# Routed experts: rows gathered for two experts at once by split products, slot weights applied in gate times up, scatter unweighted, output written in two parts

## Chip, cores and metric

The kernel runs on one core of a Trainium2 chip. The metric is the device time of one execution in microseconds (us), as the median of several runs; lower is better. One further execution is profiled, and all rows below come from it.

## What is computed

Two blocks of two layers each, on 256 rows (tokens) of 1024 channels, all in float32. The change touches only the last piece, the mixture of experts in the second layer of the second block:

```python
def moe_swiglu(h, w_router, b_router, w_gate, w_up, w_down):
    t = h.reshape(B * S, D)                                  # 256 x 1024
    logits = (t @ w_router) + b_router                       # 8 experts
    top_val, top_idx = lax.top_k(logits, TOP_K)              # 2 per row
    top_w = jax.nn.softmax(top_val, axis=-1)
    combine = jnp.sum(jax.nn.one_hot(top_idx, N_EXPERTS) * top_w[..., None], axis=1)
    out = jnp.zeros_like(t)
    for e in range(N_EXPERTS):
        out = out + combine[:, e:e + 1] * swiglu(t, w_gate[e], w_up[e], w_down[e])
    return out                                               # swiglu: (silu(h@gate) * (h@up)) @ down, width 3584

x = x + g2[:, None, :] * f                                   # f is out of above
```

## The kernel before

**Products.** Most large products are split: an operand x is kept as hi = x rounded to the type fp32r (ACT copies it) and lo = x - hi (DVE subtracts), and a product is the sum of three matrix products in that type, hi\*hi + hi\*lo + lo\*hi (`mm3`). Products of plain float32 operands are written as one `mm`; the trace has two MATMUL records for each of these and one for each product of fp32r operands.

**Weights.** They come in chunks of 1 MB through a ring (SP issues the loads, six chunks ahead). Each chunk has two halves. For a half, ACT makes `whi` (`act_split`, L954), then DVE makes `wlo` (`dve_split`, L1349), then PE multiplies. There are four buffers of halves, so ACT can start a half only when PE has finished the one four places earlier.

**The routed part** begins after the router. DVE works out for each row its two experts, its weights (`cmb`) and its place (`pos`) among the rows of each expert, at most 128 (`CAP`) an expert; the largest count decides at a branch (`fork`) whether the routed code below or the code for all rows runs. With the inputs used, the routed code runs. PE meanwhile turns the rows (`hn`, L927) and ACT copies them to `HN`. Then come the eight experts `e`, each with seven steps `f` (step n = 7e + f, 56 in all). On PE a step is, in this order:

- `hidden(n, "gate")`: 24 products of 512 columns into bank 0 or 2,
- `turn(n - 1)`: four transposes (L2015) of the hidden values of the step before,
- `hidden(n, "up")`: 24 products, into bank 1 or 3,
- what is extra in some steps: `turn_weights` in n = 2, 4, 6, 8, `scatter(e - 1)` in f = 2, `gather(e + 1)` in f = 4,
- `down(n - 1)`: 24 products into banks 4 and 5, which collect over the seven steps of an expert.

ACT does silu of gate (L2093) and the hi of the turned values (L2098), DVE multiplies by up (L2177) and makes the lo (L2170). In the first steps DVE also builds the matrices of the gather, `PSEL` (`select`, L2132: 1 where a row stands in a slot), and of the scatter, `PW` (`weigh`, L2138: the same times the weight `cmb`), which PE turns to `PWT`.

`gather(e)` picks an expert's rows: 16 float32 products of 128 columns, `HN` by `PSEL`, in two groups (banks 6 and 7); ACT makes the hi `XGH` (L2080) and DVE the lo `XGL` (L2146) of each. At the end of an expert ACT copies bank 4 and DVE bank 5 to `YS` (L2117, L2194), side by side. `scatter(e)` puts the results back in the rows' places: 8 float32 products of 256 columns, `YS` by `PWT`, in four groups that take banks 6 and 7 in turn, and DVE adds each group to `FACC` (L2154 for the first expert, L2157 after). After the last scatter DVE multiplies `FACC` by the gate of the layer and adds it to `xT` (L2198), and ACT issues four stores.

The order on each engine is the order of the code; a wait stops all that stands behind it on its engine.

## Time and profile before

| | |
|---|---|
| time, median of 3 runs | 2358.19 us (2356.99 to 2359.99) |
| the profiled execution | 2358.97 us, of which its span 2357.2 us |
| PE busy (matmul) | 2218.2 us, 94% of the span |
| DVE busy | 1784.1 us, 76% |
| ACT busy | 1393.6 us, 59% |
| the routed part | from about 1285 us to the end |
| in it, 1810 to 1940 us: PE, DVE, ACT busy | 128.8, 110.3, 93.3 of 130 us |
| there: granted PE clock, share of DMA engines, rate | 1.00, 0.87, 335 GB/s |

A row of the time line has the start (us from the span's start), the duration, the engine, the source line, the operation, what is written and what is read, and how many records are merged into the row; in square brackets stands how long the engine was idle before it and who ended that. A matrix product's record is longer than its turn on PE, as products overlap: two starts, one after the other, give the pace.

### The profile page before, as it was taken

Reading aid. Unit: us, or ns where it says so; the run is one execution under the profiler, and the core shown is the slowest. Engines: PE = TensorE matmul, PEld = TensorE weight load, DVE = VectorE, ACT = ScalarE, POOL = GpSimd, SP = SyncE. Lnnn points to the kernel's source line nnn. Section 1 sums busy time; section 2 is a strip of 40 time slices with the busy share of each in tenths; the row PEclk is TensorE's granted clock in tenths of the full one; section 3 lists DMA queues with packets and bytes.
Section 4 is the critical chain, followed back from the end, with each engine's and each line's share of the span. In section 5 each row is a group of like instructions: output and inputs, shape, how many; then the busy total and the mean of one; then the engine's idle time right before and its main releaser. Section 6 shows DMA issues by size and latency. Waiting matters only on the chain.

```text
span 2357.2 us, 31258 instructions
## 1 busy us (share of the span) xinstructions
PE 2218.2 (94%) x12766; PEld 1917.4 (81%) x12766; DVE 1784.1 (76%) x2276; ACT 1393.6 (59%) x1960; POOL 2.2 (0%) x17
## 2 busy tenths in 40 slices
PE   6989998998998988999988999999999999999998
PEld 6779998877998878999777777777777777777776
DVE  6567776756877845766846888888888888888887
ACT  4345544445544745444745767776777777776775
POOL 0000000000000000000000000000000000000000
PEclk9789999889999989999998999999999999999999
DMA  6336655434666413767413988898988888898985
GB/s 238 119 116 226 242 207 206 162 118 159 238 213 229 170 54 125 249 211 255 171 36 126 344 319 334 320 359 308 356 334 329 335 335 335 332 355 311 349 338 191
DMA packets 89428, 574.88 MB, mean 244 GB/s; under 512 B 10048, under 2 KB 10176, under 8 KB 31040
## 3 DMA queue, kind: packets, MB, share of 16 engines
q1 hardware_dynamic: 87984, 566.89, 64.4%
q0 software_dynamic: 288, 3.15, 0.4%
q10 hardware_dynamic: 1008, 2.79, 0.3%
q8 instruction: 102, 1.67, 0.3%
q14 instruction: 46, 0.38, 0.0%
HBM read 571.75 MB, written 1.05 MB: 243 GB/s over the span
## 4 chain that ended last, share of the span: by engine, by line
PE 71%; DVE 15%; ACT 10%; issue 2%; DMA 1%; SPq 0%; DVEq 0%; ACTq 0%
PE bank L458 37%; PE bank L1973 34%; DVE wlo L1349 8%; ACT whi L954 4%; DVE side L1442 2%; ACT arena L2093 1%; ACT hsh L2098 1%; DVE arena L1681 1%; DVE RSTD L1411 1%; DMA ring<-in_w_in 1%; DVE XC L1399 1%; ACT arena L1181 0%; DMA side<-in_w_ada 0%; ACT midh L1170 0%; DVE XC L1377 0%
## 5 line engine op out<-in xcount | busy, mean ns | idle before, releaser
L1349 DVE TENSOR_TENSOR wlo<-ring,whi 128x1024 fp32r<-128x1024 f32 (+1 forms) x990 | 1128.5, 1187 | 116.2 <-ACT whi L954 106.0
L954 ACT ACTIVATE whi<-ring 128x1024 fp32r<-128x1024 f32 (+1 forms) x990 | 978.0, 1028 | 179.0 <-PE bank L1973 145.2
L458 PE MATMUL bank<-HH,whi 128*128 128x256 f32 x1536 | 447.0, 291 | 18.5 <-DVE wlo L1349 11.1
L458 PE MATMUL bank<-HH,wlo 128*128 128x256 f32 x1536 | 439.1, 286 | 0.0
L458 PE MATMUL bank<-HL,whi 128*128 128x256 f32 x1536 | 438.4, 285 | 0.0
L1973 PE MATMUL bank<-whi,xgh 128*128 128x512 f32 x896 | 366.0, 409 | 8.7 <-DVE wlo L1349 0.3
L1973 PE MATMUL bank<-whi,xgl 128*128 128x512 f32 x896 | 354.5, 396 | 0.0
L1973 PE MATMUL bank<-wlo,xgh 128*128 128x512 f32 x896 | 353.8, 395 | 0.0
L458 PEld LDWEIGHTS bank<-HH,whi 128*128 128x128 f32 x1536 | 297.3, 194 | 28.2 <-issue 16.9
L458 PEld LDWEIGHTS bank<-HL,whi 128*128 128x128 f32 x1536 | 297.9, 194 | 0.5
L458 PEld LDWEIGHTS bank<-HH,wlo 128*128 128x128 f32 x1536 | 297.8, 194 | 0.0
L1973 PEld LDWEIGHTS bank<-whi,xgh 128*128 128x128 f32 x896 | 168.2, 188 | 72.0 <-DVE wlo L1349 36.7
L1973 PEld LDWEIGHTS bank<-whi,xgl 128*128 128x128 f32 x896 | 167.9, 187 | 41.2
L1973 PEld LDWEIGHTS bank<-wlo,xgh 128*128 128x128 f32 x896 | 169.0, 189 | 35.2
L1973 PE MATMUL bank<-whi,hsh 128*128 128x512 f32 x448 | 181.0, 404 | 4.9 <-DVE wlo L1349 2.4
L1973 PE MATMUL bank<-whi,hsl 128*128 128x512 f32 x448 | 177.4, 396 | 0.0
L1973 PE MATMUL bank<-wlo,hsh 128*128 128x512 f32 x448 | 176.7, 394 | 0.0
L458 PE MATMUL bank<-midh,whi 128*128 128x256 f32 x528 | 150.7, 285 | 5.7 <-DVE wlo L1349 5.5
L458 PE MATMUL bank<-midl,whi 128*128 128x256 f32 x528 | 150.1, 284 | 0.0
L458 PE MATMUL bank<-midh,wlo 128*128 128x256 f32 x528 | 150.0, 284 | 0.0
L1442 DVE SCALAR_TENSOR_TENSOR side<-side,cact 128x1024 f32<-128x1024 f32 x84 | 107.5, 1280 | 7.4 <-DMA side<-in_w_ada 6.9
L1973 PEld LDWEIGHTS bank<-whi,hsh 128*128 128x128 f32 x448 | 84.1, 188 | 30.2 <-DVE wlo L1349 9.5
(261 smaller groups left out, 2581.0 us busy)
## 6 DMA issues: line engine op xcount, KB each, us to landing
ring<-in_moe_gate SPq DMA_DIRECT2D x112, 1024.0 KB, 6.3
ring<-in_moe_up SPq DMA_DIRECT2D x112, 1024.0 KB, 5.3
ring<-in_moe_down SPq DMA_DIRECT2D x112, 1024.0 KB, 5.5
side<-in_w_ada SPq DMA_DIRECT2D x96, 512.0 KB, 4.3
ring<-in_w_up SPq DMA_DIRECT2D x44, 1024.0 KB, 4.8
ring<-in_w_in SPq DMA_DIRECT2D x32, 1024.0 KB, 5.7
ring<-in_w_down SPq DMA_DIRECT2D x32, 704.0 KB, 4.6
ring<-in_ffn_gu SPq DMA_DIRECT2D x22, 1024.0 KB, 4.8
```

Source lines behind the costliest of these rows:

```text
L458: return pe.matmul(out, lhsT, rhs, start=start, stop=stop, skip_group_check=True)
L954: a.activation(hi, part, ACT.Copy).then_inc(*made.up(("hi", n, i)))
L1349: v.tensor_tensor(lo, part, hi.bitcast(F32), ALU.subtract).then_inc(*done.up(("lo", n, i)))
L1399: v.scalar_tensor_tensor(XC[:, lo:hi, :], bc(PS[BANK[s.name, "mean"]][:, 0:S], 2), -1.0 / s.kt, XC[:, lo:hi, :], ALU.mult, ALU.add).then_i ...
L1411: v.reciprocal(RSTD[:, 0, :], RSTD[:, 0, :]).then_inc(*v_norm.up((s.name, "rstd")))
L1442: v.scalar_tensor_tensor(side_acc, side_in[n % 2], cact[:, k:k + 1], side_acc, ALU.mult, ALU.add).then_inc(*v_mod.up(("acc", n)))
L1681: v.scalar_tensor_tensor(gc[:, s:S], b[:, S:512 - s], W(f"w_fconv{l}", (2 - s) * NJ + j), gc[:, s:S], ALU.mult, ALU.add).then_inc(*v_ffn.u ...
L1973: return pe.matmul(out, lhsT, rhs, start=start, stop=stop, skip_group_check=True)
L2093: a.activation(SGB[n % 2], PS[2 * (n % 2)][:, :], ACT.Silu).then_inc(*r_act.up(("silu", n)))
L2098: a.activation(flat(HSH[(n - 1) % 2][:, :, :]), PS[BANK["turn", n - 1]][:, :], ACT.Copy).then_inc(*r_hi.up(("hst", n - 1)))
```

## The change

- **Gather**: for two experts (a pair p) at once. `HN` is kept as hi `HNH` and lo `HNL` (a new helper `low_of_rows` on DVE, in HL's space), `PSEL` is written as fp32r. A group is 4 products of fp32r operands and 256 columns (two experts wide); a pair has 4 groups g of hi (x = 0) and 4 of lo (x = 1), 32 products. ACT copies the x = 0 groups to `XG[..][0]`, DVE the x = 1 groups to `XG[..][1]`. The first pair is gathered ahead of step 0, in banks 2 to 7; pair p in steps f = 3 to 6 of expert 2p - 1, one g in each.
- **Slot weights**: 4 float32 products of one column for a pair give each slot's weight (`wsl`), which goes into the product with up (L2177 becomes a `scalar_tensor_tensor`). `weigh` and `PW` go; PE turns `PSEL` itself.
- **Scatter**: `YS` becomes hi `YSH` (ACT, both banks) and lo `YSL` (DVE, both banks, each after ACT's copy), and each of the 8 products becomes two of fp32r operands and 256 columns.
- **Output**: in step f = 4 of the last expert DVE adds `FACC` of the first seven experts to `xT`; at the end it adds the last expert's rows out of the banks, without `FACC`.
- The split `HH`, `HL` of the last normed rows is made only in the code for all rows.

```diff
+            def low_of_rows(i):
+                for g in range(2):
+                    h = slice(512 * g, 512 * g + 512)
+                    v.wait_ge(*a_rout("hn", i, g))
+                    v.tensor_tensor(HNL[:, i, h], PS[BANK["hn", i, g]][:, :], HNH[:, i, h].bitcast(F32), ALU.subtract).then_inc(
+                        *v_rout.up(("hnl", i, g)))
...
+            low_of_rows(0)
             b = PS[BANK["counts",]]
             v.wait_ge(*p_rout("counts"))
...
             v.tensor_copy(icnt[:, :], cmx).then_inc(*v_rout.up(("count",)))
+            low_of_rows(1)
...
+            def gather(p, g, x, bank=None):
+                until = [(r_vec if x else r_hi, "xg", p, g, x)]
...
+                pe.wait_ge(*r_vec("select", 2 * p + 1))
...
+                for k in range(2):
                     for i in range(2):
+                        at = 128 * (2 * g + k)
+                        tm = mm(b[:, S * k:S * k + S], (HNL if x else HNH)[:, i, at:at + 128],
+                                PSEL[:, i, 2 * p:2 * p + 2, :].rearrange("p e s -> p (e s)"), i == 0, i == 1)
+                tm.then_inc(*r_mm.up(("xg", p, g, x)))
+
+            def slot_weights(p):
+                b = take("wsl", p, until=[(r_vec, "wsl", p)])
+                for e in (2 * p, 2 * p + 1):
+                    for i in range(2):
+                        tm = mm(b[:, e % 2:e % 2 + 1], PSEL[:, i, e, :].bitcast(F32), cmb[:, i, e:e + 1], i == 0, i == 1)
...
             def scatter(e):
-                pe.wait_ge(*r_act("ys", e))
-                pe.wait_ge(*r_vec("ys", e))
                 pe.wait_ge(*r_act("pwt", 6))
                 for g in range(4):
-                    b = take("facc", e, g, until=[(r_vec, "facc", e, g)])
+                    pe.wait_ge(*r_vec("ysl", e, g // 2))
+                    b = take("facc", e, g, until=[(r_vec, "facc", e, g) if e < NE - 1 else (r_vec, "out", g)])
                     for m in range(2):
                         k = 2 * g + m
-                        tm = mm(b[:, S * m:S * m + S], YS[:, 128 * k:128 * k + 128], PWT[:, e, :], True, True)
+                        mm(b[:, S * m:S * m + S], YSH[:, 128 * k:128 * k + 128], SELT[:, e, :], True, False)
+                        tm = mm(b[:, S * m:S * m + S], YSL[:, 128 * k:128 * k + 128], SELT[:, e, :], False, True)
...
-                    if f == 4 and e + 1 < NE:
-                        gather(e + 1)
+                    if f >= 3 and e % 2 == 1 and e + 1 < NE:
+                        for x in range(2):
+                            gather((e + 1) // 2, f - 3, x)
+                        if f == END:
+                            slot_weights((e + 1) // 2)
...
-                    v.tensor_tensor(SGB[n % 2], SGB[n % 2], PS[2 * (n % 2) + 1][:, :], ALU.mult).then_inc(*r_vec.up(("hs", n)))
-                    if n < NE - 1:
+                    v.scalar_tensor_tensor(SGB[n % 2], SGB[n % 2], wsl[:, e:e + 1], PS[2 * (n % 2) + 1][:, :], ALU.mult,
+                                           ALU.mult).then_inc(*r_vec.up(("hs", n)))
+                    if 0 < n < NE - 1:
                         select(n + 1)
-                    if n < NE and n % 2 == 1:
-                        weigh(n - 1)
...
+                    if f == 4 and e == NE - 1:
+                        for m in range(8):
+                            v.wait_ge(*r_vec("facc", NE - 2, m // 2))
+                            add_out(m, FACC[:, m, :]).then_inc(*r_vec.up(("part", m)))
...
-                        v.tensor_copy(YS[:, 512:1024], PS[5][:, :]).then_inc(*r_vec.up(("ys", e)))
-            scatter(NE - 1)
+                        for h in range(2):
+                            v.wait_ge(*r_act("ysh", e, h))
+                            c = slice(512 * h, 512 * h + 512)
+                            v.tensor_tensor(YSL[:, c], PS[4 + h][:, :], YSH[:, c].bitcast(F32), ALU.subtract).then_inc(
+                                *r_vec.up(("ysl", e, h)))
```

Three places as the two programs have them. First DVE around the branch, before (`small` holds the router's values, `icnt` the count that the branch reads, `XC` is where `PSEL` lay):

```order
L1877 SCALAR_TENSOR_TENSOR small<-bank2,small 128x16
L1880 TENSOR_SCALAR small<-small 128x16
L1881 TENSOR_REDUCE small<-bank2 128x1
L1883 CAST icnt<-small 128x1
L2350 TENSOR_LOAD icnt
L2351 COMPARE_AND_BRANCH
L2132 TENSOR_SCALAR XC<-cst,small 128x128 x2
L1349 TENSOR_TENSOR wlo<-ring,whi 128x1024 x2
```

and now (`HL` holds `HNL`):

```order
L1862 TENSOR_TENSOR HL<-bank6,hnh_67 128x512
L1862 TENSOR_TENSOR HL<-bank7,hnh_67 128x512
L1899 SCALAR_TENSOR_TENSOR small<-bank2,small 128x16
L1905 CAST icnt<-small 128x1
L1862 TENSOR_TENSOR HL<-bank0,hnh_67 128x512
L1862 TENSOR_TENSOR HL<-bank1,hnh_67 128x512
L2417 TENSOR_LOAD icnt
L2418 COMPARE_AND_BRANCH
L2178 TENSOR_SCALAR psel_59<-cst,small 128x128 x4
L1362 TENSOR_TENSOR wlo<-ring,whi 128x1024 x2
```

Two subtractions stand ahead of the count's work, two ahead of the branch, and four rather than two selections behind it.

On PE ahead of step 0, between the branch and the first product of gate (bank 0), before:

```order
L2351 COMPARE_AND_BRANCH
L1973 MATMUL bank6<-XC,arena 128x128 x8
L1973 MATMUL bank7<-XC,arena 128x128 x8
L1973 MATMUL bank0<-whi,xgh0_51 128x512
```

and now:

```order
L2418 COMPARE_AND_BRANCH
L1997 MATMUL bank2<-psel_59,hnh_67 128x256 x4
L1997 MATMUL bank3<-psel_59,hnh_67 128x256 x4
L1997 MATMUL bank4<-psel_59,HL 128x256 x4
L1997 MATMUL bank5<-psel_59,HL 128x256 x4
L1997 MATMUL bank6<-psel_59,hnh_67 128x256 x4
L1997 MATMUL bank7<-psel_59,hnh_67 128x256 x4
L1997 MATMUL bank6<-psel_59,HL 128x256 x4
L1997 MATMUL bank7<-psel_59,HL 128x256 x4
L1997 MATMUL bank6<-small,psel_59 128x1 x4
L1997 MATMUL bank0<-whi,xg0_55 128x512
```

All 32 products of the first pair and the four of the slot weights stand ahead of step 0; bank 6 is taken three times and bank 7 twice.

On DVE in step f = 4 of the last expert, now (before, no `xT` row stands there):

```order
L1362 TENSOR_TENSOR wlo<-ring,whi 128x1024 x4
L2227 SCALAR_TENSOR_TENSOR arena<-arena,small,bank3 128x512
L2203 SCALAR_TENSOR_TENSOR xT<-arena,modT,xT 128x256 x8
L1362 TENSOR_TENSOR wlo<-ring,whi 128x1024 x2
L1362 TENSOR_TENSOR wlo<-ring_2_65,whi 128x1024 x4
```

The eight additions stand between the product with up and the lo half of the second chunk of down.

## Rows read from the trace of the kernel before

**Rows 1.** Waits from 1290 us on: engine line, who ended it: us, times, longest.

```profile
PEld bank L1973 <- DVE wlo L1349: 46.2, 78, 1.1
```

**Rows 2.** Chain that ended last, 2300 us on: start us, us, what.

```profile
2306.47 0.60 ACT arena L2093
...
2308.53 1.24 DVE wlo L1349
...
2309.81 14.30 PE bank L1973 x60
...
2324.14 0.60 ACT arena L2093
```

**Rows 3.** Time line of PE: the transposes of steps 8 to 11.

```profile
1460.49 0.60 PE L2015 MATMUL bank<-cst,arena 128*128 128x128 f32 x4
...
1481.80 0.60 PE L2015 MATMUL bank<-cst,arena 128*128 128x128 f32 x4
...
1499.43 0.60 PE L2015 MATMUL bank<-cst,arena 128*128 128x128 f32 x4
...
1521.02 0.60 PE L2015 MATMUL bank<-cst,arena 128*128 128x128 f32 x4
```

**Rows 4.** Time line: a gather, on PE and ACT (step 11).

```profile
1505.87 3.73 PE L1973 MATMUL bank<-XC,arena 128*128 128x128 f32 x32
...
1507.86 0.60 ACT L2080 ACTIVATE xgh<-bank 128x512 fp32r<-128x512 f32 x1 [3.35 <-PE bank L1973]
```

**Rows 5.** Time line of PE: pace of fp32r products of 256 columns, full and half clock.

```profile
1256.58 0.28 PE L458 MATMUL bank<-HH,whi 128*128 128x256 f32 x1
...
1256.70 0.28 PE L458 MATMUL bank<-HL,whi 128*128 128x256 f32 x1
...
1246.48 0.41 PE L458 MATMUL bank<-HH,whi 128*128 128x256 f32 x1
1246.69 0.41 PE L458 MATMUL bank<-HL,whi 128*128 128x256 f32 x1
```

**Rows 6.** Time line: a scatter, on PE and DVE (step 9).

```profile
1466.95 3.80 PE L1973 MATMUL bank<-arena 128*128 128x256 f32 x16
...
1467.30 0.68 DVE L2177 TENSOR_TENSOR arena<-arena,bank 128x512 f32<-128x512 f32 x1
1468.01 0.69 DVE L2154 COPY arena<-bank 128x512 f32<-128x512 f32 x1
```

**Rows 7.** Time line: an early step (n = 1), PE's transposes and DVE's weighing.

```profile
1308.74 0.60 PE L2015 MATMUL bank<-cst,arena 128*128 128x128 f32 x4
...
1327.36 0.60 PE L2015 MATMUL bank<-cst,arena 128*128 128x128 f32 x4
...
1316.54 1.11 DVE L2138 TENSOR_SCALAR SQ<-cst,small 128x128 f32<-128x128 f32 x4
```

**Rows 8.** Time line: an expert's end, ACT and DVE.

```profile
1568.57 0.60 ACT L2117 ACTIVATE arena<-bank 128x512 f32<-128x512 f32 x1 [1.73 <-PE bank L1973]
1569.06 3.89 ACT L954 ACTIVATE whi<-ring 128x1024 fp32r<-128x1024 f32 x4
...
1570.14 4.63 DVE L1349 TENSOR_TENSOR wlo<-ring,whi 128x1024 fp32r<-128x1024 f32 x4 [0.89 <-ACT whi L954]
```

**Rows 9.** Time line of the start; last row a stretch: us, busy us by engine, granted clock, DMA.

```profile
1285.42 0.48 DVE L2132 TENSOR_SCALAR XC<-cst,small 128x128 f32<-128x128 f32 x2 [0.72 <-DVE icnt L1883]
...
1286.05 5.33 PE L1973 MATMUL bank<-XC,arena 128*128 128x128 f32 x32 [2.03 <-DVE XC L2132]
1291.14 0.48 PE L1973 MATMUL bank<-whi,xgh 128*128 128x512 f32 x1
...
1286.00:1288.00 2.00, 1.95 (x9) 1.98 (x10) 1.54 (x2) 1.37 (x2) 0.00 (x0) 0.50 0.82 344
```

**Rows 10.** Time line of DVE at the end.

```profile
2343.97 0.69 DVE L2194 COPY arena<-bank 128x512 f32<-128x512 f32 x1 [3.40 <-PE bank L1973]
...
2349.32 3.25 DVE L2198 SCALAR_TENSOR_TENSOR xT<-arena,modT,xT 128x256 f32<-128x256 f32 x8
```

More of the change, by code:

```diff
@@ L162, in build @@
         XGL = [over(f"xgl{i}", 10240 + 1024 * i, 8, 128) for i in range(2)]
+        XG = [[over(f"xg{i}", 8192 + 2048 * i, 8, 2, 128) for i in range(2)],
+              [nc.alloc_sbuf_tensor_at("xg_hh", [128, 8, 2, 128], F32R, offset=HH_at),
+               nc.alloc_sbuf_tensor_at("xg_ht", [128, 8, 2, 128], F32R, offset=hT_at)]]
+        PSEL = nc.alloc_sbuf_tensor_at("psel", [128, 2, NE, 128], F32R, offset=hT_at + 4 * 2048)
+        YSL = nc.alloc_sbuf_tensor_at("ysl", [128, 1024], F32R, offset=hT_at + 4 * 4096)
         HSH = [over(f"hsh{i}", 12288 + 512 * i, 4, 128) for i in range(2)]
@@ L924, in pe_program @@
                 for g in range(2):
-                    b = take("hn", i, g, until=[(a_rout, "hn", i, g)])
+                    b = take("hn", i, g, until=[(v_rout, "hnl", i, g)])
                     for k in range(4):
@@ L1203, in rms_modulated @@
                 a.wait_ge(*v_norm(s.name, "amod"))
-                affine(s, hT, lambda k: amod[:, which, k:k + 1], lambda k: modT[:, l, sh + k:sh + k + 1])
+                affine(s, hT, lambda k: amod[:, which, k:k + 1], lambda k: modT[:, l, sh + k:sh + k + 1],
+                       then=(which, l) == (1, 1))
             for l in range(DEPTH):
@@ L1712, in rms_modulated @@
                 norm_finish(s)
-                low_parts(s)
+                if (which, l) != (1, 1):
+                    low_parts(s)
             def gated_residual(l, which, m, b, name):
@@ L2028, in down @@
                 if f == 0:
-                    for signal, *end in ([(r_act, "ys", e - 1), (r_vec, "ys", e - 1)] if e > 0 else tail[4] + tail[5]):
+                    for signal, *end in ([(r_vec, "ysl", e - 1, 0), (r_vec, "ysl", e - 1, 1)] if e > 0 else tail[4] + tail[5]):
                         pe.wait_ge(*signal(*end))
@@ L2073, in ahead, with gather @@
                     act_split(a, n + 1, used=in_use(r_w), made=r_hi)
-            def gather(e):
-                for g in range(2):
-                    a.wait_ge(*r_mm("xg", e, g))
-                    if e >= 2:
-                        a.wait_ge(*r_w("up", NFB * (e - 1) - 1))
-                    a.activation(flat(XGH[e % 2][:, 4 * g:4 * g + 4, :]), PS[BANK["xg", e, g]][:, :], ACT.Copy).then_inc(
-                        *r_hi.up(("xg", e, g)))
+            def gather(p, g):
+                a.wait_ge(*r_mm("xg", p, g, 0))
+                if p >= 2:
+                    a.wait_ge(*r_w("up", 2 * NFB * (p - 1) - 1))
+                a.activation(XG[p % 2][0][:, 2 * g:2 * g + 2, :, :].rearrange("p k e s -> p (k e s)"),
+                             PS[BANK["xg", p, g, 0]][:, :], ACT.Copy).then_inc(*r_hi.up(("xg", p, g, 0)))
             act_split(a, first_moe, used=in_use(r_w), made=r_hi)
-            gather(0)
+            for g in range(4):
+                gather(0, g)
             for n in steps:
@@ L2157, in scatter, with add_out @@
                         v.tensor_tensor(dst, dst, b[:, :], ALU.add).then_inc(*r_vec.up(("facc", e, g)))
+            def add_out(m, rows):
+                return v.scalar_tensor_tensor(xT[:, m, :], rows, modT[:, 1, 40 + m:41 + m], xT[:, m, :], ALU.mult, ALU.add)
             select(0)
+            select(1)
             dve_split(v, first_moe, made=r_hi, done=moe_lo["r"])
-            gather(0)
+            for g in range(4):
+                gather(0, g)
+            slot_weights(0)
             for n in steps:
@@ L2261, in ahead @@
                     act_split(a, n + 1, used=in_use(d_w), made=d_hi)
+            a.wait_ge(*a_norm(("rms1", 1), "dst", 7))
+            for k in range(0, 8, 2):
+                a.activation(HH[:, k:k + 2, :], hT[:, k:k + 2, :], ACT.Copy).then_inc(*d_hi.up(("hh", k)))
             act_split(a, first_moe, used=in_use(d_w), made=d_hi)
@@ L2289, in ahead @@
                     dve_split(v, n + 1, made=d_hi, done=moe_lo["d"])
+            v.wait_ge(*v_rout("hnl", 1, 1))
+            for k in range(0, 8, 2):
+                v.wait_ge(*d_hi("hh", k))
+                v.tensor_tensor(HL[:, k:k + 2, :], hT[:, k:k + 2, :], HH[:, k:k + 2, :].bitcast(F32), ALU.subtract).then_inc(
+                    *d_vec.up(("hl",)))
             dve_split(v, first_moe, made=d_hi, done=moe_lo["d"])
```

96 lines of the change are left out of this document (54 added, 42 removed).

## The prediction

> **What bounds the kernel now.** Start with the shares of the routed part (table of the profile): PE is busy 128.8 of 130 us at the full clock, DVE 110.3, ACT 93.3, so what PE does there, and what PE waits for, is the time. The view of waits then says what PE waits for: DVE's lo halves, 46.2 us in 78 times [rows 1], and no row names a load. The chain shows where: in a step with nothing extra, silu starts at 2306.47 behind gate's last product, ACT then makes two more tiles, DVE makes the lo half from 2308.53, and PE goes on at 2309.81, about 0.3 us later than it could [rows 2]. This chain hangs on ACT and is left alone by the change. The next silu is at 2324.14: a plain step takes 17.67 us. Step lengths are then read from one step's transposes to the next: the step with a scatter 21.31, a plain one 17.63, the one with a gather 21.59 [rows 3]. So a scatter costs 3.65 us and a gather 3.93, all on PE, and the DMA engines at a share of 0.87 are not asked for more than in plain steps, whatever the others become.
>
> **The price of the new products.** A float32 gather is 16 products, 32 records, 3.73 us up to the last one's end, 0.11 us a record [rows 4]. The new products have fp32r operands, each its own stationary tile, and 256 columns. That form exists in the trace: 0.12 us from start to start at the full clock, 0.21 at half [rows 5]. I take 0.12, the same form; the bounds are 0.11 (the record above) and, upwards, twice 0.12, which is left to a rival.
>
> **Gathers, -11.4.** Removed are the seven in the steps, at 3.93 each: 27.5 us. Added are three pairs of four steps. In each of these steps PE does 8 products, 0.96 us. Who is late next? PE wants the second chunk of down 12 products of 512 columns later (60 records take 14.30 us in [rows 2], of which four are transposes; 0.234 each), so 0.96 + 2.81 = 3.77 us after up. ACT now copies a gather's tile ahead of that chunk's hi. An engine starts 0.35 us after PE's turn is over (1467.30 against 1466.95, [rows 6]), so ACT at 0.48 + 0.35 = 0.83; 0.5 for the copy (the step from 1568.57 to 1569.06, [rows 8]), 1.06 for the hi, 1.22 for DVE's lo: ready at 3.65. It just fits, so no gap. In f = 6 the slot weights come on top: their bank is free when ACT's copy ends (1.43), 8 records of 0.11 follow, and 0.2 for the change of type: 2.5 us instead of 0.96. A pair costs 3 x 0.96 + 2.5 = 5.4, three cost 16.1. Bounds: 13 (records hidden, no bank wait) and 21 (a gap of 0.3 in each step).
>
> **Scatters, -5.0.** Sixteen products would be 1.92 us, but four groups share two banks and DVE empties them. Before, DVE begins the product with up 0.35 us after the scatter's start, the first bank at 1.06, and is done with it at 1.75 [rows 6]. The third group can't begin earlier, whatever its products cost: 1.78 to 2.26. The second bank is empty at 2.39, the fourth group takes 2.43 to 2.91. So a scatter costs 2.9 instead of 3.65; down's lo is then ready at 5.2 and wanted at 5.7. Seven times 0.72. Bounds: -12 (no wait for banks) and -3.
>
> **Early steps, -3.4.** Step 1 takes 18.62; in it and in steps 3, 5 and 7 DVE weighs for 1.11 us between the product with up and down's second lo [rows 7], and PE waits. Without it three of them become plain (0.95 each); step 7 also holds an expert's end and gives 0.54. Steps 2, 4, 6 and 8 keep their transposes.
>
> **Ends of experts, +3.5.** Before, ACT and DVE copied one bank each at 1568.57, ACT went on with the hi of gate at 1569.06, DVE with its lo at 1570.14 [rows 8], and PE waited for that lo a little (0.37 us is what such a step takes more). Now ACT copies both, so its hi starts 0.5 later, and everything behind with it; DVE's two subtractions end before that hi does. Seven ends of 0.5. Bounds 0.3 (the copy's pace less slack) and 1.0 (DVE late as well).
>
> **The product with up** becomes another instruction of DVE with a scalar: one more operand, same columns; I take 0, bounds 0 and 0.1, and 0.8 us of slack cover it.
>
> **The last expert, +2.75.** Eight additions, 3.25 us [rows 10], now stand in step 53 between the product with up (ends 1.03 after up) and down's second lo. That is ready at 1.05 + 3.24 + 1.22 = 5.5, wanted at 2.81. Nothing covers them there; before they stood at the very end.
>
> **The start, +3.9.** `low_of_rows(0)`, 1.3 us, fits into DVE's idle time before the counts. `low_of_rows(1)`, another 1.3, stands before the branch, and four selections (0.95) instead of two (0.48) behind it. By the Trainium skill, Perfetto Trace Analysis, section on the DVE / Act engine instruction, the sequencer goes on as soon as an instruction is pushed into the wait queue. By it the load and the branch (0.72 us of idle time in [rows 9]) would run under the subtractions and the start would lie about 0.5 us earlier than with both in a row. From the rows alone: PE's first gather product comes 1.05 to 1.8 us later than 1286.05; I take 1.35, 1287.4. Before, PE had been idle 2.03 us, ran at the clock 0.50 (1.2 of 2.4 GHz) from there [rows 9] and took 5.1 us up to gate at 1291.14. Now it idles longer and has 32 products. At 0.21 each the first 24 take until 1292.5; then banks 6 and 7 must be emptied by ACT, filled again at 0.12, emptied by DVE, and the slot weights (0.9) done: gate begins at 1295.3. That is 4.2 later, less 0.26 for a wait for lo that disappears there: 3.9. Bounds 2.7 (full clock after 2 us) and 6 (half clock all along).
>
> **The end, -2.9.** From the copies at 2343.97 to the last write of `xT` at 2352.57 [rows 10] are 8.6 us. Now: ACT 0.6, DVE's first lo until 1.31, first group 1.45 to 1.93, two additions until 3.16, third group (it needs the first one's bank) 3.2 to 3.68, fourth until 4.48, last addition until 5.73. The stores behind it are the same.
>
> **Sum.** -11.4 - 5.0 - 3.4 + 3.5 + 2.75 + 3.9 - 2.9 = -12.55 us. The profiled execution took 2358.97 (its span 2357.2 and 1.8 around it), so 2346.4; the median of the runs lies 0.8 below that execution: **2345.6**. A measurement of this kernel can tell about 0.2%, 4.7 us.
>
> **Rivals.**
> *Banks don't hold the scatter* (PE works at its own pace, 2.0 us each): a further 6.3 us gained, 2339.3. Against it stands DVE's start at 1468.01. 0.06.
> *ACT and DVE take over.* The slack in a gather step is 0.1 us and an expert's end has none. If ACT's copy comes 0.5 later than I put it, 12 steps lose 0.4 and seven ends another 0.6: +9, 2355, no change that can be told. For it: PE already waits 78 times for lo. Against it: ACT is idle 3.35 us before a gather's tile [rows 4]. 0.11, about half of it below the bound for faster.
> *The small products cost twice, and the kernel is slower.* The mechanism: the load of each product's own stationary tile isn't hidden behind only 256 columns, so a product takes 0.24 at the full clock and 0.43 at half. Twelve gather steps get 0.96 longer (11.5), seven scatters take 3.84 instead of 2.9 (6.6), gate's first product comes 3.4 later, the end 0.9: +22.4, 2368. The gain is used up at about 0.2 us a product. Against it stand the records 0.12 us apart, of the same shapes, with a tile of its own each [rows 5]. 0.05. By the Trainium skill, TensorE: Matmul & The Clock Gate, section LDWEIGHTS (loading the stationary operand), 128 columns take 107 ns to load; one after the other with 256 columns that would be an estimated 0.216 us a product and about 2362 in all. [Rows 5] show 0.12, so the trace speaks for loads that are hidden.
>
> **Chances and range.** Forecast 0.78, rivals 0.06, 0.11, 0.05. The likeliest case alone spans 2341 to 2351, its widest terms being gathers (3 to 5 us), scatters (2 to 7) and the start (1 to 2), taken together as independent. With part of the second rival: 2340.5 to 2352.5. Faster (below 2353.5, that is by over 0.2%): 0.78 + 0.06 + 0.04 = 0.88; same 0.07; slower 0.05.
>
> **What would show it.** Step lengths between transposes: scatter steps near 20.6, gather steps 18.6 and that with slot weights 20.2, plain ones 17.66, the end of an expert 18.5, step 53 near 20.4 (17.66 + 2.75). Records of the new products 0.12 us apart. Gate's first product near 1295, its clock 0.50 before 1292. From the last copy's start to the last write of `xT` 5.7 us. I am wrong if gather steps show a gap in down, if scatter steps fall to 19.7, or if gate starts after 1297.

## The result, and the profile after

| | before | after |
|---|---|---|
| time, median of 5 runs | 2359.99 us (2356.99 to 2360.77) | 2347.17 us (2345.44 to 2347.66) |
| the profiled execution: own time, span | 2358.97, 2357.2 us | 2347.09, 2344.6 us |
| router's sum (DVE's first read of the logits) | 1278.59 | 1278.71 |
| from there to the end of the span | 1078.6 | 1065.9 |

The ratio after to before is 0.9948, its 95% interval 0.9933 to 0.9962: faster by 0.4 to 0.7%; the medians lie 12.8 us apart. The forecast was 2345.6, with a range from 2340.5 to 2352.5. Two runs at a much lower clock (2727.38 us of one experiment, 3115.38 of the kernel before) are in no median, ratio or range of this document.

First the view of waits from 1290 us on (engine line, who ended it: us, times, longest), of the kernel after.

```profile
PEld bank L1997 <- DVE wlo L1362: 45.1, 70, 2.9
PE bank L1997 <- DVE wlo L1362: 10.9, 36, 2.5
...
PEld bank L1997 <- DVE arena L2200: 5.1, 6, 0.9
PE bank L1997 <- DVE arena L2200: 3.9, 6, 0.7
```

PE's weight loads (PEld) still wait for lo halves as long as in [rows 1], but one wait is now 2.9 us long where the longest was 1.1. PE's own waits for them have grown to 10.9 us (2.7 us in 6 before): 2.5 is one wait in step 53, seven of 0.57 to 0.59 stand at the ends of experts, and the other 28 are of 0.15, in steps that are no longer for it. And there is a wait for the bank that DVE's additions of a scatter hold. Step lengths come from PE's transposes, as in [rows 3]: here the transposes of steps 8 to 14, and of steps 52 to 54.

```profile
1457.42 0.60 PE L2055 MATMUL bank<-cst,arena 128*128 128x128 f32 x4
1477.99 0.60 PE L2055 MATMUL bank<-cst,arena 128*128 128x128 f32 x4
1496.59 0.60 PE L2055 MATMUL bank<-cst,arena 128*128 128x128 f32 x4
1515.19 0.60 PE L2055 MATMUL bank<-cst,arena 128*128 128x128 f32 x4
1533.79 0.60 PE L2055 MATMUL bank<-cst,arena 128*128 128x128 f32 x4
1553.76 0.60 PE L2055 MATMUL bank<-cst,arena 128*128 128x128 f32 x4
1572.23 0.60 PE L2055 MATMUL bank<-cst,arena 128*128 128x128 f32 x4
...
2274.65 0.60 PE L2055 MATMUL bank<-cst,arena 128*128 128x128 f32 x4
...
2296.35 0.60 PE L2055 MATMUL bank<-cst,arena 128*128 128x128 f32 x4
2313.97 0.60 PE L2055 MATMUL bank<-cst,arena 128*128 128x128 f32 x4
```

The scatter's step takes 20.57 us, three gather steps 18.60 each, the fourth, with the slot weights, 19.97, an expert's end 18.47. Step 53 takes 21.70, and the next one is plain again, 17.62. A gather on PE's time line (step 11) shows eight products in 0.95 us, and no gap behind them:

```profile
1503.05 0.64 PE L1997 MATMUL bank<-psel,hnh 128*128 128x256 f32 x4
...
1503.53 0.64 PE L1997 MATMUL bank<-psel,HL 128*128 128x256 f32 x4
...
1504.00 0.39 PE L1997 MATMUL bank<-whi,hsh 128*128 128x512 f32 x1
```

A scatter (step 9): products 0.12 apart within a group, then a wait of 0.66 us for the bank.

```profile
1464.57 0.28 PE L1997 MATMUL bank<-selt,ysh 128*128 128x256 f32 x1
1464.69 0.28 PE L1997 MATMUL bank<-selt,ysl 128*128 128x256 f32 x1
1465.63 0.39 PE L1997 MATMUL bank<-selt,ysh 128*128 128x256 f32 x1 [0.66 <-DVE arena L2197]
```

The start, PE's time line, and the granted clock (last number but two of a stretch) in it:

```profile
1286.84 2.08 PE L1997 MATMUL bank<-psel,hnh 128*128 128x256 f32 x8 [2.71 <-DVE psel L2178]
1288.71 1.91 PE L1997 MATMUL bank<-psel,HL 128*128 128x256 f32 x8
...
1293.97 1.05 PE L1997 MATMUL bank<-small,psel 128*128 128x1 f32 x8 [0.22 <-DVE xg L2185]
1294.89 0.48 PE L1997 MATMUL bank<-whi,xg 128*128 128x512 f32 x1
```

```profile
1284.00:1286.00 2.00, 0.13 (x2) 0.04 (x1) 1.77 (x7) 0.52 (x1) 0.00 (x0) 0.99 1.02 430
1286.00:1288.00 2.00, 1.16 (x5) 1.16 (x6) 2.00 (x6) 1.48 (x2) 0.00 (x0) 0.50 0.84 356
1288.00:1290.00 2.00, 2.00 (x12) 2.00 (x11) 1.25 (x2) 1.20 (x2) 0.00 (x0) 0.50 0.00 0
```

Gate's first product comes 16.18 us behind the router's sum (1294.89 less 1278.71), where it was 12.55. PE idles 2.71 us instead of 2.03, works at the clock 0.50 (1.2 GHz) from its first product on, and eight products take 1.7 to 1.9 us there. At the end, DVE's last writes of `xT`:

```profile
2336.21 1.66 DVE L2203 SCALAR_TENSOR_TENSOR xT<-bank,modT,xT 128x256 f32<-128x256 f32 x4 [0.24 <-PE bank L1997]
2338.44 1.73 DVE L2203 SCALAR_TENSOR_TENSOR xT<-bank,modT,xT 128x256 f32<-128x256 f32 x4 [0.56 <-PE bank L1997]
```

### The profile page after: what moved, and what is told of

Same layout as the page of the kernel before. It is cut to its first block, busy times and chain, and to the rows that moved or that the text cites. A ratio compares the mean times of both kernels' runs of the same rounds, so it can differ in the third digit from the quotient of the medians.

```text
span 2344.6 us, 31073 instructions
## 1 busy us (share of the span) xinstructions
PE 2198.4 (94%) x12670; PEld 1904.8 (81%) x12670; DVE 1786.1 (76%) x2276; ACT 1393.6 (59%) x1964; POOL 2.2 (0%) x17
## 3 DMA queue, kind: packets, MB, share of 16 engines
HBM read 571.75 MB, written 1.05 MB: 244 GB/s over the span
## 4 chain that ended last, share of the span: by engine, by line
PE 71%; DVE 16%; ACT 10%; issue 2%; DMA 1%; SPq 0%; DVEq 0%; ACTq 0%
PE bank L470 37%; PE bank L1997 33%; DVE wlo L1362 8%; ACT whi L966 4%; DVE side L1455 2%; ACT arena L2138 1%; ACT hsh L2143 1%; DVE arena L1694 1%; DVE RSTD L1424 1%; DMA ring<-in_w_in 1%; DVE XC L1412 1%; ACT arena L1193 0%; ACT ysh L2163 0%; DMA side<-in_w_ada 0%; ACT midh L1182 0%
## 5 line engine op out<-in xcount | busy, mean ns | idle before, releaser
L1997 PE MATMUL bank<-whi,xg 128*128 128x512 f32 x896 | 301.2, 402 | 5.7 <-DVE wlo L1362 1.7
L1997 PEld LDWEIGHTS bank<-whi,xg 128*128 128x128 f32 x896 | 168.1, 188 | 57.4 <-DVE wlo L1362 19.2
L1997 PE MATMUL bank<-whi,xg_hh 128*128 128x512 f32 x448 | 182.7, 408 | 6.7 <-DVE wlo L1362 6.7
L1997 PE MATMUL bank<-wlo,xg_hh 128*128 128x512 f32 x448 | 177.1, 395 | 0.0
L1997 PE MATMUL bank<-wlo,xg 128*128 128x512 f32 x448 | 176.9, 395 | 0.0
L1997 PE MATMUL bank<-whi,xg_ht 128*128 128x512 f32 x448 | 176.4, 394 | 0.0
L1997 PEld LDWEIGHTS bank<-whi,xg_hh 128*128 128x128 f32 x448 | 84.1, 188 | 38.0 <-DVE wlo L1362 20.5
```

What stands on the lines that cost most here:

```text
L1997: return pe.matmul(out, lhsT, rhs, start=start, stop=stop, skip_group_check=True)
```

## The experiments

All start from the kernel after; differences are against it, while ratios, with their 95% intervals, are to the kernel before, run beside each. Code cuts show the main lines; `...` stands where lines are left out. The code ahead of the router's sum is the same in all of them, yet in the profiled executions that sum comes between 1277.5 and 1293.9 us, so a span alone says little about a difference of 4 us. Every reading of a profile below is therefore counted from the router's sum to the end of the span (the row of DVE that reads the logits).

| | router's sum | from there to the end | against after | gate's first product behind the sum |
|---|---|---|---|---|
| after | 1278.71 | 1065.9 | | 16.18 |
| additions in idle time | 1281.84 | 1061.8 | -4.1 | 16.19 |
| additions in two steps | 1279.15 | 1064.5 | -1.4 | 16.17 |
| banks emptied in idle time | 1281.99 | 1058.2 | -7.7 | 16.18 |
| scatter's third bank | 1278.03 | 1061.7 | -4.2 | 16.18 |
| scatter in float32 | 1278.63 | 1065.6 | -0.3 | 16.18 |
| output in one part | 1277.49 | 1063.7 | -2.2 | 16.18 |
| gather products halved | 1286.64 | 1082.2 | +16.3 | 23.51 |
| gather in float32, in pairs | 1279.36 | 1077.8 | +11.9 | 17.01 |
| products that nothing reads | 1293.87 | 1062.5 | -3.4 | 13.86 |
| four moves | 1278.29 | 1049.9 | -16.0 | 16.15 |
| four moves, and those products | 1290.57 | 1047.7 | -18.2 | 13.87 |

### The gather: is it the pairing or the split?

The pairs stay, but the rows are gathered by float32 products, 16 for four tiles, and split behind them, as before the change:

```diff
...
-                        tm = mm(b[:, S * k:S * k + S], (HNL if x else HNH)[:, i, at:at + 128],
-                                PSEL[:, i, 2 * p:2 * p + 2, :].rearrange("p e s -> p (e s)"), i == 0, i == 1)
+                        tm = mm(b[:, S * k:S * k + S], HN[:, i, at:at + 128],
+                                PSEL[:, i, 2 * p:2 * p + 2, :].rearrange("p e s -> p (e s)").bitcast(F32), i == 0, i == 1)
...
```

> Edit: only the split of the gather is undone, the pairs stay: HN is a float32 copy, four float32 products of 256 columns in a group, ACT makes the hi and DVE the lo of the gathered rows as before; the router part has no lo of rows. Theory (a float32 product of 256 columns takes 0.43 us, so a gather step has 1.72 us of products and 0.2 for the change of type, and the tile that ACT must copy comes later by as much): gather steps go from 18.6 to 19.8, those with slot weights from 19.97 to 20.5, gate's first product comes about 2 us later; 14 us more, 2361. Rival (pairing carries the gain, the split little): under 5 us more.

Measured: 2359.07 us median, ratio to the kernel before 1.0006 (0.9987 to 1.0025). Gather steps 19.74, with slot weights 20.26. One row of PE (step 11 of that kernel) has the price:

```profile
1505.73 1.89 PE L1995 MATMUL bank<-psel,arena 128*128 128x256 f32 x8
```

Four products of 256 columns in float32 are eight records and 1.9 us up to the last one's end; the split form does the same rows in 0.95 from start to start. With the split undone the gain is gone: this kernel, with all its other changes, stands where the kernel before did. That doesn't yet say that the split would gain without pairs, and this is what the next run asks.

Then each split product is cut into two of 128 columns, one expert each. This kernel leaves out that the sums must be right: both halves of a bank are now under way at once, and its results are not those of the others. Only times are read from it; number, shapes and order of its instructions are as the cut says.

```diff
-                        tm = mm(b[:, S * k:S * k + S], (HNL if x else HNH)[:, i, at:at + 128],
-                                PSEL[:, i, 2 * p:2 * p + 2, :].rearrange("p e s -> p (e s)"), i == 0, i == 1)
+                        for w in range(2):
+                            tm = mm(b[:, S * k + 128 * w:S * k + 128 * w + 128], (HNL if x else HNH)[:, i, at:at + 128],
+                                    PSEL[:, i, 2 * p + w, :], i == 0, i == 1)
```

> Edit: the gather keeps its split, its groups and its places, but each product of 256 columns (two experts) becomes two of 128 columns with the same stationary tile written out twice: 64 products a pair instead of 32. Theory (a product of 128 columns takes no less than the load of its stationary tile, 0.11 us, the record of the float32 gather): a gather step has 16 products at 0.11, 1.75 us instead of 0.96, so 18.6 becomes 19.4 in twelve steps, and gate's first product comes 4 us later; about 13 us more, 2360. Rival (time goes by columns): 0.06 a product, no change.

Measured: one run, 2371.66 us. Gather steps 19.40 to 19.45, 0.84 more, with slot weights 20.33, 0.36 more. PE's time line (a gather, and the start):

```profile
1501.73 1.00 PE L1997 MATMUL bank<-psel,hnh 128*128 128x128 f32 x8
1502.57 1.06 PE L1997 MATMUL bank<-psel,HL 128*128 128x128 f32 x8
```

```profile
1294.77 3.67 PE L1997 MATMUL bank<-psel,hnh 128*128 128x128 f32 x16 [2.71 <-DVE psel L2179]
1298.24 3.62 PE L1997 MATMUL bank<-psel,HL 128*128 128x128 f32 x16
...
1308.48 1.81 PE L1997 MATMUL bank<-small,psel 128*128 128x1 f32 x8
```

Eight products of 128 columns take 0.84 us, 0.105 each, against 0.12 with 256 columns; at half clock sixteen take 3.4, 0.21 each, and those of 256 columns took the same. The slot weights' records, of one column, take no less: eight in 0.92 us in the kernel after (1293.97 to 1294.89), in 1.67 at half clock here (1308.48 to 1310.15). So the columns hardly count at this size: each product, with its stationary tile, has a floor of about 0.105 us at the full clock and 0.21 at half. By the Trainium skill, TensorE: Matmul & The Clock Gate, section LDWEIGHTS (loading the stationary operand), the load takes the number of columns divided by 1.2, in ns, an estimated 107 ns for 128 columns. At the full clock the pace agrees with that load alone, not with load and product in a row; at half clock the floor of 0.21 is twice the page's figure, and the measurement decides. The rival that the small products cost twice is thereby gone.

Twice as many at half clock also explain the start: 64 times 0.21 are 13.6 us, the slot weights 1.7, and gate began 15.4 behind the first of them, 7.3 later than in the kernel after. The clock still stood at 0.50 behind gate's start, here in the stretch from 1312 to 1314 us, and the way from there to the first transposes took 2.0 longer.

```profile
1312.00:1314.00 2.00, 2.00 (x6) 1.61 (x5) 0.75 (x1) 0.85 (x1) 0.00 (x0) 0.50 0.31 49
```

The two runs together answer the question. The rows of two experts cost PE four gather steps; over plain steps and without slot weights these are 4 times 0.95, 3.8 us, in the kernel after, 4 times 2.09, 8.4, with pairs in float32, and 4 times 1.79, 7.2, with split products of 128 columns, where two gathers of the kernel before cost 7.9. (Pairing also moves one expert's gather out of the steps and ahead of them.) So neither half of the change gains much alone. Two split products of 128 columns (0.21) cost as much as one float32 product of 128 (two records of 0.11, [rows 4]); only at 256 columns, where a split product costs 0.12, do two of them take half of a float32 one.

### The scatter: do the banks hold it?

The third group of a scatter goes into the bank of gate's sum, which silu has read by then. The gate two steps later, which uses this bank next, now waits for DVE's addition (left out of the cut).

```diff
...
+                    if g == 2 and e < NE - 1:
+                        i = 2 * ((7 * (e + 1) + 2) % 2)
+                        pe.wait_ge(*r_act("silu", 7 * (e + 1) + 2))
+                        b = PS[i]
...
```

> Edit: in the seven scatters inside the steps the third group goes to the bank of gate, free since silu, instead of waiting for bank 6 or 7; the fourth waits for the first group's bank. Theory (a scatter is held by banks that DVE has to empty, not by its 16 products): PE takes groups one to three in a row (1.44 us) and the fourth from 1.78 to 2.26, so scatter steps fall from 20.57 to 19.9, seven times 0.65, 4.5 us less. Rival (the products themselves take the 2.9 us): scatter steps stay at 20.57.

Measured: one run, 2342.24 us, -4.2 from the router's sum on; scatter steps 19.95 to 19.99. The wait of 0.66 us between the second and the third group is gone, 0.18 remain before the fourth:

```profile
1464.49 0.28 PE L1997 MATMUL bank<-selt,ysl 128*128 128x256 f32 x1
1464.95 0.39 PE L1997 MATMUL bank<-selt,ysh 128*128 128x256 f32 x1 [0.18 <-DVE arena L2205]
```

Seven times 0.60 are 4.2: the two banks held the scatter, as the prediction's sum had it. (Step 53 took 0.2 longer in this execution and the stretch behind the last transposes was 0.4 shorter, so that the total agrees so well is in part chance.)

Next, the scatter goes back to float32, with one copy on ACT and one on DVE at an expert's end:

```diff
...
-                        mm(b[:, S * m:S * m + S], YSH[:, 128 * k:128 * k + 128], SELT[:, e, :], True, False)
-                        tm = mm(b[:, S * m:S * m + S], YSL[:, 128 * k:128 * k + 128], SELT[:, e, :], False, True)
+                        tm = mm(b[:, S * m:S * m + S], YSH[:, 128 * k:128 * k + 128].bitcast(F32), SELT[:, e, :].bitcast(F32),
+                                True, True)
...
```

> Edit: only the split of the scatter is undone: ACT copies bank 4 and DVE bank 5 in float32 side by side, and the scatter is 8 float32 products again (unweighted, and the output still in two parts). Theory (the split gains 0.72 us a scatter and costs 0.45 us an expert's end): scatter steps go from 20.57 to 21.3, ends of experts from 18.48 to 18.03, the last scatter changes little, together +2 us, about 2349. Rival (the split is worth the ratio of the products' own times, 3.45 to 1.92 us, and its ends cost nothing): +10 us, 2357.

Measured: 2349.08 us median, ratio 0.9958 (0.9939 to 0.9977); scatter steps 21.27, ends 18.0. That is +0.70 seven times and -0.47 seven times. With step 53 at 20.40 instead of 21.70 (below) the profile shows -0.3 in all, so without that step +1.0: the split of the scatter, as a whole, gained 1 to 1.6 us of the 12.8.

### The ends of experts

ACT's two copies and DVE's two subtractions move from behind the splits of down to the idle time ahead of the hi and lo of the transposes, one step later:

```diff
...
+                    if n > 1:
+                        empty(n - 1)
                     if n >= 2:
...
-                        for h in range(2):
-                            a.activation(YSH[:, 512 * h:512 * h + 512], PS[4 + h][:, :], ACT.Copy).then_inc(
-                                *r_act.up(("ysh", e, h)))
+                    if n == len(seq):
+                        empty(n)
...
```

> Edit: the emptying of banks 4 and 5 at an expert's end (two copies on ACT, two subtractions on DVE) moves one step later, to where ACT waits 1.75 us for the last product of gate and DVE 1.6 us for ACT's tile; the last expert's stays. Theory (an end costs 0.83 us only because the copies stand ahead of the hi of the next weights): the steps of an expert's end fall from 18.48 to 17.65, seven times 0.83, 5.8 us less, about 2341. Rival (the two subtractions, 1.29 us, make DVE late wherever they stand, or the copies delay silu): those steps, or the ones behind, stay at 18.2 or more, under 2 us gained.

Measured: 2340.11 us median of three, ratio 0.9909 (0.9889 to 0.9930). All seven ends take 17.63 to 17.66, as plain steps do, instead of 18.47 to 18.52: -5.9. Most of the rest of the -7.7 is step 53, 20.43 in this execution. So the work itself is free; its place cost 0.84 us at each end, part of it already before the change (18.0).

### The last expert's additions

```diff
...
+                if n < len(seq) and seq[n][0] == NE - 1 and 3 <= seq[n][1] <= 5:
+                    for m in range(3 * (seq[n][1] - 3), min(8, 3 * (seq[n][1] - 2))):
+                        v.wait_ge(*r_vec("facc", NE - 2, m // 2))
+                        add_out(m, FACC[:, m, :]).then_inc(*r_vec.up(("part", m)))
                 if n > 0:
...
-                    if f == 4 and e == NE - 1:
-                        for m in range(8):
...
```

> Edit: the eight additions of FACC to xT move from behind the product with up in step 53 (21.6 us long in the changed kernel, a plain step 17.65) to the places in steps 52, 53 and 54 where DVE waits 1.6 us for ACT's tile, ahead of the lo of the turned values: three, three and two of them, 0.41 us each. Theory (the cost of step 53 is DVE's lateness and what the late lo half does to PE, and idle time on DVE is a cover): steps 52, 53 and 54 all take 17.65, the whole 4.0 us comes back, about 2343. Rival (the additions cost their own 3.25 us wherever they stand, as DVE is nearly full): the three steps together stay about 3 us above plain ones, 2346.

Measured: 2346.52 us median, ratio 0.9944 (0.9926 to 0.9962). Steps 52, 53 and 54 take 17.64, 17.62, 17.64: the full 4.1 us come back behind the router's sum. The median shows 0.7 of it, and in the profiled execution the part ahead of the sum took 3.1 us longer. The runs of this kernel spread over 5.3 us, the longest at the lowest mean clock (0.957 against 0.961); that this is the part ahead of the sum in all of them is argued, as each kernel has one profile.

Then the same additions, four in step 53 and four in step 54, behind the product with up:

```diff
-                    if f == 4 and e == NE - 1:
-                        for m in range(8):
+                    if f in (4, 5) and e == NE - 1:
+                        for m in range(4 * (f - 4), 4 * (f - 3)):
```

> Edit: the same place as in the changed kernel, but four additions in step 53 and four in step 54. Theory (in step 53 the long idle time of PE also lets its granted clock fall to 0.50, and products at that clock make up about 1.2 of the 4.0 us): each of the two steps has lo ready at 1.05 + 1.62 + 1.22 = 3.9 us after up, wanted at 2.81, so 1.1 us of idle time each, the clock stays 1.00, both steps take about 18.75, together 2.2 above plain ones: 1.8 less than in the changed kernel. Rival (no part of the clock; a fixed price per addition on PE's path): together 3.9 to 4.0 above plain ones, as now.

Measured: one run, 2345.85 us; the two steps take 18.84 and 18.81, +2.4 together, with the clock at 1.00. Eight additions in one place cost 2.8 or 4.1, in two places 2.4, in three idle ones nothing.

Last, the output in one part, as before: all eight additions behind the last scatter.

```diff
...
-                add_out(m, PS[BANK["facc", NE - 1, m // 2]][:, S * (m % 2):S * (m % 2) + S]).then_inc(*r_vec.up(("out", m // 2)))
+                v.wait_ge(*r_vec("facc", NE - 1, m // 2))
+                add_out(m, FACC[:, m, :]).then_inc(*r_vec.up(("out", m // 2)))
```

> Edit: only the output in two parts is undone: no additions in step 53, the last expert's rows are added to FACC and then all eight additions to xT follow. Theory: step 53 becomes plain (21.6 to 17.65, 4.0 us less), the stretch from the last copy's start to the last write of xT grows by 2.7 us, so 1.2 us less in all, 2346: the two parts were a loss where they stand. Rival (additions in step 53 cost nothing at the full clock and the end is what counts): 2.7 us more, 2350.

Measured: one run, 2343.7 us. Step 53 is plain, 17.63 (-4.07), and from the last product of down to the end there are 12.9 us instead of 11.05 (+1.8, where +2.7 was expected). Where it stood in the change, the output in two parts lost 2.2 us; in an execution whose step 53 takes 20.43 (below) it would be an estimated 1.0 (2.8 less 1.8).

### The clock at the start

PE gets 20 products that nothing reads, between the counts and the fork:

```diff
...
             mm(b[:, 16:24], ones, msk[:, 1, :], False, True).then_inc(*p_rout.up(("counts",)))
+            b = take("warm", until=[])
+            pe.wait_ge(*a_rout("hn", 0, 0))
+            for _ in range(20):
+                mm(b[:, 0:256], HNH[:, 0, 0:128], HNH[:, 0, 0:256], True, True)
```

> TensorE gets 20 products that nothing reads behind the counts, 0.12 us each, so that it idles 0.4 us instead of 2.7 ahead of the first gather. Theory (the start's price is mostly the clock: PE idles, the granted clock is 0.50 from 1286 on, and the 32 gather products and the slot weights take 0.21 and more each): gate's first product comes 13.5 us behind the router's sum instead of 16.2 (in four executions it was 16.18), since 24 products shrink from 0.21 to 0.12 (2.2) and the slot weights by 0.5. Rival (the copies of ACT and DVE hold PE at the start, whatever the clock): 15.8 to 16.2, the clock at 1.00 all the same. Second rival (the clock falls in spite of the products, for what PE did before): 16.2 with 0.50. Nothing else changes: step 53 stays 20.4 or 21.7.

Measured: one run, 2359.07 us, with the router's sum at 1293.87, 15 us later than in the kernel after; from there to the end it is 3.4 us faster. PE's time line, and a stretch:

```profile
1299.14 2.63 PE L470 MATMUL bank<-hnh 128*128 128x256 f32 x20
1301.99 1.21 PE L2001 MATMUL bank<-psel,hnh 128*128 128x256 f32 x8 [0.22 <-DVE psel L2182]
1303.04 1.10 PE L2001 MATMUL bank<-psel,HL 128*128 128x256 f32 x8
...
1307.73 0.48 PE L2001 MATMUL bank<-whi,xg 128*128 128x512 f32 x1
```

```profile
1302.00:1304.00 2.00, 2.00 (x17) 2.00 (x18) 2.00 (x2) 1.73 (x3) 0.00 (x0) 1.00 0.31 131
```

The idle time ahead of the gather falls from 2.71 to 0.22 us, the clock stays at 1.00, eight products take 0.95 to 1.05 instead of 1.7 to 1.9, and gate begins 13.86 behind the router's sum instead of 16.18. The first gather product stands 8.12 behind the sum, where it was 8.13, so the 2.3 us are the clock alone. How much of the start's 3.6 they explain stays open, since the kernel before had a stretch at 0.50 here too ([rows 9]) and no run took that away. Two short waits for ACT's and DVE's copies (0.22 and 0.29) are what those hold. Step 53 took 20.43 here, which is about the rest of the 3.4 us.

### The moves together

Additions, emptying and third bank as above, and the slot weights of a pair five steps earlier, in f = 1 and no longer in f = 6:

```diff
...
-                        if f == END:
-                            slot_weights((e + 1) // 2)
+                    if f == 1 and e % 2 == 1 and e + 1 < NE:
+                        slot_weights((e + 1) // 2)
...
```

> Four moves together: the last expert's eight additions and the emptying of down's banks stand in DVE's and ACT's idle time ahead of the hi and lo of the transposes, the third group of a scatter goes into gate's bank, and the slot weights of a pair are made in the step f = 1. Added up from single runs: -4.0, seven ends -5.8, seven scatters -4.2, slot weights -1.2 (from 2.3 to 0.9 in three steps would be -4, but the records still take PE 0.9 each; only the wait for a bank and for DVE goes): -15.2 counted from the router's sum to the end, so 1050.7 instead of 1065.9, and a median near 2332. Rival (the moves take one another's cover: ACT's and DVE's idle time is used twice): some 4 us less, 2336. Steps: ends of experts 17.64, scatters 19.97, gather steps 18.6, step 53 17.64.

Measured: 2330.17 us median (2328.69 to 2335.81), ratio 0.9875 (0.9847 to 0.9903). From the router's sum 1049.9, where 1050.7 was expected: ends 17.64 to 17.66, scatters 19.95 to 19.99, the fourth gather step 18.6, step 53 17.64, and 0.5 to 0.9 for the slot weights in their new steps. The moves don't take each other's cover.

> The four moves and the 20 products that nothing reads together. Theory (start's clock and steps are separate): another 2.7 us below the four moves alone, all of it between the router's sum and gate's first product: 1048.0 from the sum to the end, median near 2329.5. Rival (copies hold the start, or the clock falls all the same): as the four moves alone within 0.5 us.

Measured: 2330.38 us median (2325.16 to 2340.06), ratio 0.9863 (0.9834 to 0.9892). From the sum to the end 1047.7, 2.2 less than with the four moves alone, all of it at the start (13.87). The medians don't tell the two kernels apart; the profile does. Both beat the kernel before, and the kernel after too: their intervals lie below its 0.9933 to 0.9962.

## Why the prediction was right, and where it wasn't

**The bound.** PE's products and what PE waits for set the time: -13.4 over the 55 steps, +3.3 up to the first transposes, -2.6 behind the last; together -12.7 from the router's sum on, where the forecast change was -12.55. That the total comes so near is partly luck: the last expert cost 1.3 more than forecast, and the gathers and the start 0.6 each less. The time itself came 1.6 above the forecast because the kernel before, run again, had a median 1.8 higher (2359.99 against 2358.19).

**The price of the products** was right: 0.12 us. The halved products show that this is close to the floor of one, 0.105, and so that the 256 columns carry the gain as much as the split does; the prediction didn't say so.

**Gathers**, forecast -11.4: 0.9 to 1.0 each in nine steps, 2.3 in three, against six gathers of 3.93 and one of 3.59 (step 4), together -12.0. Slot weights cost 1.4 where I had 1.5. The 0.2 for the change of type in that term stood without a row; behind float32 gathers the first fp32r product of 512 columns holds PE for 0.31 us (before) and 0.42 (float32 in pairs), where the next ones take 0.23, so 0.1 to 0.2.

**Scatters**, forecast -5.0: seven times 0.72 (21.29 to 20.57), -5.0, held by the banks as worked out.

**Early steps and ends**, forecast -3.4 and +3.5: steps 1, 3 and 5 are plain (17.64, 17.66, 17.67; -2.85), step 7 comes out even, six ends cost 0.46 on average (18.47 to 18.52). Together -0.1, where +0.1 was forecast. That it is the weighing that kept steps 1, 3, 5 and 7 long is read from the steps; no run put it back.

**The end**, forecast -2.9: from the last copies to the last write of `xT` 6.18 us (2333.99 to 2340.17), not 5.73, against 8.6 before. The third and fourth group came at half clock, after PE had waited. With the stores -2.6.

**The start**, forecast +3.9: +3.6 up to gate, and 0.36 come back within step 0 where I had 0.26, so +3.3. The row of the first gather, 1286.84, lies 0.79 behind [rows 9]: below my lower bound of 1.05. DVE's selections started at 1285.92, directly behind the second pair of subtractions:

```profile
1284.72 1.28 DVE L1862 TENSOR_TENSOR HL<-bank,hnh 128x512 fp32r<-128x512 f32 x2
1285.92 0.86 DVE L2178 TENSOR_SCALAR psel<-cst,small 128x128 fp32r<-128x128 f32 x4
```

So the load of the count and the branch, 0.72 us of idle time in [rows 9], ran under the subtractions. That is what the sentence of the Trainium skill (Perfetto Trace Analysis, the section on the DVE / Act engine instruction) gave, which I had named and not used: with it, 0.5 off my 1.35 are 0.85, and 0.79 was measured.

**The last expert** is the term that was mis-sized: +2.75 forecast, +4.0 measured. Up to PE's restart the sum held: PE waited 2.50 us, where I had 5.5 less 2.81. Missing was what a wait of 2.5 us can do to the clock. Here are the kernel after, PE's time line and the granted clock:

```profile
2286.56 0.79 PE L1997 MATMUL bank<-whi,hsh 128*128 128x512 f32 x1 [2.50 <-DVE wlo L1362]
2287.15 0.63 PE L1997 MATMUL bank<-wlo,hsh 128*128 128x512 f32 x1
2287.58 0.63 PE L1997 MATMUL bank<-whi,hsl 128*128 128x512 f32 x1
```

```profile
2285.00:2287.00 2.00, 0.44 (x1) 0.44 (x2) 2.00 (x3) 0.16 (x1) 0.00 (x0) 0.77 0.48 188
2287.00:2289.00 2.00, 2.00 (x6) 1.52 (x6) 2.00 (x3) 0.00 (x0) 0.00 (x0) 0.50 0.27 45
```

and, in the kernel whose banks are emptied in idle time, the same place:

```profile
2283.80 0.50 PE L1997 MATMUL bank<-whi,hsh 128*128 128x512 f32 x1 [2.51 <-DVE wlo L1362]
2284.14 0.40 PE L1997 MATMUL bank<-wlo,hsh 128*128 128x512 f32 x1
```

```profile
2283.00:2285.00 2.00, 1.20 (x5) 1.03 (x6) 2.00 (x3) 0.00 (x0) 0.00 (x0) 1.00 0.01 4
```

The idle time is the same, 2.50 and 2.51 us. In the first the next six starts are 0.42 to 0.59 us apart, in the second 0.23 to 0.34. Step 53 took 21.70, 21.94 and 21.96 in three profiles and 20.40 to 20.43 in four others: two values, 1.3 to 1.6 apart. The lower one is the forecast's 20.4, so the term was right for four profiles of seven, and which of the two an execution gets was not settled. At the start I had counted the clock, because [rows 9] show it at 0.50; in the middle of the routed part it stood at 1.00, and I didn't ask what the new wait would do to it.

Of the rivals, banks that don't hold the scatter fell with the third-bank run, the doubled product with the halved one; the copies of ACT and DVE that take over are seen only at the ends of experts, at the size that was forecast, and in no gather step. The chance of 0.88 for faster rested on the gather, and there the margin was large.

## What to carry to other kernels

A float32 product of 256 columns that only picks rows can be exchanged for two split ones, which together take half of PE's time. At 128 columns the exchange gains next to nothing, as a split product then costs almost as much as at 256; so the products must be made wide, here by pairing experts, and split, and neither alone paid. Where side work stands in an engine's order counts for more than its length: additions, emptying of banks, slot weights and a third bank, moved without changing any of the work, gained 16.0 us, more than the whole change (12.7). A new wait of PE of about 2.5 us should be priced twice, as itself and with another 1.3 to 1.6 us for half clock behind it, which is what it cost here in three executions of seven.

## What the runs showed of the hardware

- A split product of 128 columns costs almost as much as one of 256: 0.105 and 0.12 us at the full clock, 0.21 and 0.21 at half.
- After the same idle time of PE the granted clock was 0.50 in one execution (2.50 us) and 1.00 in another (2.51 us).
- The part ahead of the router's sum, the same code everywhere, took 1277.5 to 1293.9 us. Its granted clock goes with it. Here are the stretches from 400 to 850 us, first of the kernel after (sum at 1278.71), then of the one with the unread products (1293.87):

```profile
400.00:850.00 450.00, 417.39 (x2845) 387.56 (x2844) 320.27 (x510) 220.02 (x396) 0.99 (x6) 0.94 0.51 180
```

```profile
400.00:850.00 450.00, 418.08 (x2784) 385.73 (x2783) 317.95 (x508) 219.65 (x397) 1.00 (x6) 0.91 0.50 178
```

  PE is busy for as long, but at 0.91 instead of 0.94, and gets 61 products less done. With the moves and those products, spans of one kernel ran from 2323.4 (mean clock 0.964) to 2338.3 us (0.956). What decides it stays open. By the spread of the runs it limits what a median of a few can tell here to an estimated 3 us, and counting from a fixed row inside the profile is what made differences of 1 us readable.
- The time outside the span differed by kernel and hardly by run: 1.8 to 1.9 us in every run of the kernel before, of the one with banks emptied in idle time, with the scatter in float32 and of the last two, 2.3 to 2.9 in all the others, the kernel after among them. So 0.7 us of the 12.6 that the span lost were not seen in the time. What those with the short one have in common is that ACT's two copies don't stand behind the splits of down inside the steps; whether that is the cause was not tried.
